# A two-block transformer kernel: the tail of the second block's mixing product, the query products of its expert layer and the first expert choice, reordered

## Chip, core and metric

The kernel runs on one core of a Trainium2 chip. The metric is the device time of one execution in microseconds. The engines are TensorE (PE), VectorE (DVE), ScalarE (ACT), GpSimd (POOL) and SyncE (SP); in the profile PEld is TensorE's loading of the stationary operand, which runs beside its products.

## What is computed

Two transformer blocks over 256 tokens of width 1024, in fp32. The change lies in the second block, from its output product on:

```
x = x + mixed @ w_out
hn = _rmsnorm(x, norm2_g)
q = (hn @ peer_wq).reshape(tokens, 8 heads, 256)
s1 = q[..., :128] . peer_keys[0]        # 128 scores
s2 = q[..., 128:] . peer_keys[1]        # 128 scores
v1, i1 = top_k(s1, 16);  v2, i2 = top_k(s2, 16)
cand_s = v1[:, None] + v2[None, :]      # 16 x 16 sums
top_s, pos = top_k(cand_s, 16)
e = i1[pos // 16] * 128 + i2[pos % 16]
g = softmax(top_s)
h = gelu(x . peer_u[e])
out = sum(g * h * peer_v[e])
x = x + out;  return _rmsnorm(x, final_g)
```

For each token and head 16 of 16384 experts are chosen, and for each of them a row of 1024 numbers of `peer_u` and one of `peer_v` are read from DRAM: 2 x 16 rows for each of 256 x 8 pairs, 268 MB in all.

## The kernel before

Tokens lie in two tiles of 128 (t = 0, 1), one token on a partition. All weights of the dense products come as granules of 1 MB (128 x 2048 fp32) through a ring of three slots: SP loads granule n into `raw[n % 3]`, ACT writes its high part `w_hi` (`prepare`, L1126), POOL writes the rest `w_lo` (`low_part`, L1998, in four pieces), and PE makes three fp32r products for one fp32 product: high x high, low x high, high x low (`mm3`, L612 to L614, and `by_parts`, L701 and L705). A slot is loaded again when its low part is written.

The output product of the second block uses four granules, `wp0` to `wp3` (`half_sum`), each for both token tiles; q is the granule, q % 2 the output half and q // 2 the half of the inner dimension. `wp2` and `wp3` also wait for the convolution branch (`conv_out`, written by DVE L1814). Results go to PSUM banks, DVE adds them to `X` (`residual`, L1458), PE transposes `X` (`raw_turn`, L681), DVE multiplies by the gain (L1451), ACT takes the high part (L1135) and DVE the low part (L1443).

Then follow eight query products, one for each head (`pair`, granules `wq0` to `wq7`, 48 products of 256 columns each), ACT's copy of each to `query` (L1320, L1326), the key scores (`score_tile`, L982) and ACT's copy of these to `match`. The low parts of the last five granules are made by DVE (`late_split`, L1931), all others by POOL.

A group g is one head of one token tile; there are 16, tile 0 first. For each, DVE chooses 16 experts (`choose_first` for group 0, `choose` for the others; the indices are written at L1872 and L1896), POOL issues 16 indirect DMAs for rows of `peer_u` and 16 for rows of `peer_v` (L2036, each fetches one 4 KB row for each of 128 tokens, 0.52 MB), in batches m = 0 to 7 of two rows, DVE makes the dot products with the u rows (L1913, 16 for a group), ACT the gelu and 16 diagonal matrices of weights (L1353, L1360), and PE adds the weighted v rows (L1008, 32 fp32 products of 512 columns, shown as 64 records). u rows and v rows have one buffer each: a u batch is fetched again when DVE has used it (`u_free`), a v batch when PE has (`v_free`).

POOL's order decides when rows come: u rows of group 0, u rows of group 1, then, after the last query product, v rows of group 0; from there on a loop over groups g = 2 to 15 with, for each m, the u batch of group g and the v batch of group g - 1. The first u batches of the loop wait for the choice of group 2, which DVE makes in the midst of the dot products of group 1.

## Time and profile before

| | us |
|---|---|
| median of 3 runs | 1361.41 |
| lowest and highest of them | 1357.44, 1363.77 |
| the profiled execution | 1354.4 |
| its span, first to last instruction | 1352.6 |
| mean granted clock of TensorE | 0.886 of 2.4 GHz |
| busy: PE, DVE, ACT, POOL | 1101.4, 714.1, 419.0, 895.2 |
| moved by all DMA | 356.86 MB, of it 268.47 MB by POOL's indirect DMAs |

All times in the rows below count from the start of the span, 1352.6 us long; 1.8 us of the execution lie around it. POOL's 512 indirect DMAs run from 571.5 to 1315.8 us, more than half of the span. A row of a timeline gives start, duration, engine, line, operation, output <- input, count, and in brackets the idle time before it with what ended it; "issue" and "remote" there mean that the profile shows nothing that it waited for. An fp32 product appears as two records, an fp32r product as one.

### The profile page before, as it was taken

To read this page: it belongs to the slowest core of one execution; us is meant where nothing else is said; L and a number is where in the kernel's file an instruction comes from. 1 tells how busy PE (TensorE), PEld (TensorE's weight loads), DVE (VectorE), ACT (ScalarE), POOL (GpSimd) and SP (SyncE) were. 2 spreads that over 40 slices of the span, in tenths; PEclk is the share of its full clock that TensorE was granted. 3 is DMA by queue.
4 is the path that set the end of the run, shared out by engine and by line. 5 is a ranking of instruction groups with operands and counts; after the bars stand their busy time and mean duration, and the time that the engine had idled before them with its cause. 6 is when DMAs were issued, how large, how long until landed. Compare 5 with 4: busy or idle time off the path is not lost.

```text
span 1352.6 us, 14212 instructions
## 1 busy us (share of the span) xinstructions
PE 1101.4 (81%) x4814; PEld 735.0 (54%) x4814; DVE 714.1 (53%) x1600; ACT 419.0 (31%) x761; POOL 895.2 (66%) x845
## 2 busy tenths in 40 slices
PE   6999999999999998996858757766877776686757
PEld 5778898999988877893313313322333232232322
DVE  6436222222263786594646567746665664572842
ACT  4355454444435445534202202220222022012202
POOL 5764448788897675686565757666766666765670
PEclk9999889999999999997988879768977877887878
DMA  7533225555554312499799999999999999989891
GB/s 253 182 129 121 77 84 187 171 178 179 179 190 179 109 48 100 161 373 350 304 389 350 365 370 366 352 352 408 348 346 360 382 359 350 411 339 366 310 410 65
DMA packets 89442, 356.86 MB, mean 264 GB/s; under 512 B 9648, under 2 KB 9776, under 8 KB 81840
## 3 DMA queue, kind: packets, MB, share of 16 engines
q0 software_dynamic: 73728, 268.47, 51.5%
q1 hardware_dynamic: 15232, 86.15, 17.9%
q10 hardware_dynamic: 432, 1.57, 0.4%
q8 instruction: 32, 0.52, 0.2%
q14 instruction: 18, 0.15, 0.0%
HBM read 355.10 MB, written 1.05 MB: 263 GB/s over the span
## 4 chain that ended last, share of the span: by engine, by line
PE 15%; DVE 12%; issue 10%; another core or an unknown queue 8%; POOL 3%; DMA 1%; ACT 1%; DVEq 0%; ACTq 0%; POOLq 0%
PE bank L1008 14%; DVE u_row L1913 7%; POOL v_row L2036 2%; POOL u_row L2036 2%; DMA v_row<-peer_v_dram,expert 1%; DVE gain L1843 1%; ACT diag L1360 1%; DVE gain L1894 0%; DVE c_part L1895 0%; DVE gain L1892 0%; DVE c_pos L1850 0%; DVE s_idx L1846 0%; DVE s_idx L1850 0%; DVEq L1392 0%
## 5 line engine op out<-in xcount | busy, mean ns | idle before, releaser
L1008 PE MATMUL bank<-v_row,diag 128*128 128x512 f32 x960 | 500.4, 669 | 197.2 <-issue 156.4
L1998 POOL TENSOR_TENSOR w_lo<-raw,w_hi 128x512 fp32r<-128x512 f32 x296 | 375.7, 1303 | 155.4 <-ACT w_hi L1126 155.0
L1008 PEld LDWEIGHTS bank<-v_row,diag 128*128 128x128 f32 x960 | 200.9, 212 | 496.4 <-issue 453.9
L1913 DVE CUSTOM_DVE_ANT_0 u_row<-u_row,bank 128x1024 f32<-128x1024 f32 x256 | 298.5, 1218 | 63.6 <-issue 52.3
L2036 POOL DMA_INDIRECT u_row<-peer_u_dram,expert x256 | 248.7, 972 | 113.5 <-issue 78.3
L2036 POOL DMA_INDIRECT v_row<-peer_v_dram,expert x240 | 226.7, 945 | 138.9 <-issue 67.3
L612 PE MATMUL bank<-hT_hi,w_hi 128*128 128x256 f32 x672 | 194.7, 290 | 5.2 <-issue 1.8
L614 PE MATMUL bank<-hT_hi,w_lo 128*128 128x256 f32 x672 | 192.6, 287 | 5.7 <-issue 5.7
L613 PE MATMUL bank<-hT_lo,w_hi 128*128 128x256 f32 x672 | 192.5, 286 | 2.4 <-issue 2.3
L1126 ACT ACTIVATE w_hi<-raw 128x2048 fp32r<-128x2048 f32 x79 | 150.9, 1911 | 109.0 <-PE bank L614 64.7
L1353 ACT ACTIVATE gelu<-dots 128x16 f32<-128x16 f32 x16 | 3.5, 216 | 476.5 <-DVE dots L1913 221.1
L612 PEld LDWEIGHTS bank<-hT_hi,w_hi 128*128 128x128 f32 x672 | 131.5, 196 | 10.9 <-issue 8.0
L614 PEld LDWEIGHTS bank<-hT_hi,w_lo 128*128 128x128 f32 x672 | 131.3, 195 | 5.2 <-issue 5.2
L613 PEld LDWEIGHTS bank<-hT_lo,w_hi 128*128 128x128 f32 x672 | 131.6, 196 | 1.3 <-issue 1.3
L1360 ACT ACTIVATE diag<-consts,mixw 128x128 f32<-128x128 f32 x256 | 77.3, 387 | 83.0 <-remote 55.7
L1708 DVE TENSOR_TENSOR full<-full,bank 128x512 f32<-128x512 f32 x11 | 7.6, 688 | 102.9 <-PE bank L614 102.9
L701 PE MATMUL bank<-w_hi,hT_hi 128*128 128x512 f32 (+2 forms) x128 | 46.4, 374 | 6.8 <-DVE hT_lo L1443 2.9
L701 PE MATMUL bank<-w_hi,hT_lo 128*128 128x512 f32 (+2 forms) x128 | 45.9, 370 | 0.0
L1882 DVE COPY gain<-match 128x256 f32 (+1 forms) x15 | 4.8, 322 | 74.1 <-remote 37.3
L1458 DVE TENSOR_TENSOR residual<-residual,bank 128x512 f32<-128x512 f32 x12 | 8.2, 684 | 61.5 <-PE bank L614 31.8
L612 PE MATMUL bank<-w_hi,ff_hi 128*128 128x512 f32 x88 | 34.3, 390 | 0.9 <-issue 0.9
L613 PE MATMUL bank<-w_lo,ff_hi 128*128 128x512 f32 x88 | 34.2, 389 | 0.0
(259 smaller groups left out, 1333.4 us busy)
## 6 DMA issues: line engine op xcount, KB each, us to landing
raw<-stream_dram SPq DMA_DIRECT2D x79, 1024.0 KB
u_row<-peer_u_dram,expert POOLq DMA_INDIRECT x256
v_row<-peer_v_dram,expert POOLq DMA_INDIRECT x240
residual<-x_in_dram SPq DMA_DIRECT2D x2, 512.0 KB, 4.6
out_dram<-residual SPq DMA_DIRECT2D x4, 256.0 KB, 2.1
consts<-consts_in_dram SPq DMA_DIRECT2D x1, 840.0 KB, 13.5
gain<-norm_final_dram ACTq DMA_DIRECT2D x1, 512.0 KB, 7.5
normed_tokens<-norm_g_dram ACTq DMA_DIRECT2D x1, 512.0 KB, 3.5
```

The lines of the kernel that those rows point to most:

```text
L612: mm(out_ap, left[0], right[0], start=first, stop=False, skip_group_check=resumed)
L613: mm(out_ap, left[0], right[1], start=False, stop=False, skip_group_check=resumed)
L614: return mm(out_ap, left[1], right[0], start=False, stop=last, skip_group_check=resumed)
L701: mm(outs[t], x[:, k, t * P:(t + 1) * P], w, start=first and k == chunks[0] and x is source[0], stop=False)
L1008: ins = mm(accs[half][:, :], diag[:, 2 * m + i, :], row[:, half * 512:(half + 1) * 512], start=False, stop=True, skip_group_check=True)
L1126: activation(w_hi[n % RING][:, :], raw[n % RING][:, :], ACT.Copy).then_inc(high_done, 1)
L1360: ins = activation(diag[:, i, :], ident, ACT.Copy, scale=mixw[:, i:i + 1])
L1458: ps.empty(v.tensor_tensor(part, part, bank[:, :], ALU.add), (name, t, half))
L1843: ins = v.match_replace(left, top[:, 0:8], values, TAKEN)
L1913: ins = v.tensor_tensor_reduce(out=row_of_u, in0=row_of_u, in1=hn_tile[:, :], scale=1.0, scalar=0.0, op0=ALU.mult, op1=ALU.add, accum_out= ...
L1998: ins = nc.gpsimd.tensor_tensor(w_lo[r][:, cols], raw[r][:, cols], w_hi[r][:, cols].bitcast(F32), ALU.subtract)
L2036: nc.gpsimd.indirect_dma_start(rows[2 * m + i][:, :], None, table_in, bass.IndirectOffsetOnAxis(ap=expert[:, b, 2 * m + i:2 * m + i + 1], ...
```

## The change

- **Order of the output product.** The pieces of `wp0` to `wp3` are now one for each granule and token tile. Those of tile 0 come first, with only `wp1`'s piece for tile 1 split around the transposes of tile 0. Norm, first query product and key scores of tile 0 stand between pieces of tile 1.
- **`wp3`'s high and low part** have a fourth slot, and ACT makes the high part just after the attention, ahead of the square root of the convolution branch.
- **Query products unsplit.** Granules `wq0` to `wq7` are neither split by ACT nor by POOL or DVE. PE multiplies fp32 weights with an fp32 `hT_whole`: 16 products of 128 columns for one head and tile (heads 0 and 1, `query_of_tile`), 16 of 256 columns for both tiles (heads 2 to 7, `query_of_head`). Each granule has a place of its own, and SP loads all before the first rows of experts are fetched.
- **First choice.** Group 0's first eight experts come from the sums of the eight best of each list (8 x 8 instead of 16 x 16). The first index is ready as soon as the two lists of eight are (`best_expert`), seven more after that, and the other eight after a residual addition of tile 1.
- **Gathers.** POOL begins with one u row, then one and fourteen more; v rows of group 0 for m = 0 and 1 come ahead of group 1's u rows, those for m = 2 to 7 behind, each batch m when the query product of head m is done (its weights lay there).
- **ACT's weights of group 0** (`expert_weights(0)`) stand between heads 4 and 5, and no longer behind head 7; DVE chooses group 2 as soon as the scores of head 2 are copied, and makes the dot products of group 1 after that without a break.

```
-LATE = 5
+NSPLIT = GRANULES.index("wq0")
...
-            for n in range(RING, NGRAN):
-                late = n - RING - (NGRAN - LATE)
...
+            for n in range(RING, NSPLIT):
+                sp.wait_ge(split_done, n - RING + 1)
                 load(n)
+                if GRANULES[n] == "wp2":
+                    ps.full(sp, ("conv", 3))
+                    load_query(5)
+            for h in range(RING):
+                sp.wait_ge(split_done, NSPLIT + h - RING + 1)
+                load_query(h)
+            sp.wait_ge(part_read, PARTIAL.index("wp0") + 1)
+            for h in (3, 4):
+                load_query(h)
+            sp.wait_ge(conv_out, 2)
+            for h in (6, 7):
+                load_query(h)
...
+            tile_of_out(0, 0)
+            partly_read("wp0", tile_of_out(0, 1))
+            ps.start(pe, ("out2", 0, 1))
+            tile_of_out(1, 0)
+            pe.wait_ge(conv_out, 2)
+            ps.fill(tile_of_out(2, 0), ("out2", 0, 0))
+            ps.fill(tile_of_out(3, 0), ("out2", 0, 1))
+            turn_of_out(0, 0)
+            ps.start(pe, ("out2", 1, 1))
+            out_products(1, 1, "high", range(2))
+            turn_of_out(0, 1)
+            query_of_tile(0, 0, fresh=True)
+            out_products(1, 1, "high", range(2, 4))
+            tile_scores(0, 0)
+            partly_read("wp1", out_products(1, 1, "low"))
+            ps.fill(tile_of_out(2, 1), ("out2", 1, 0))
+            ps.fill(tile_of_out(3, 1), ("out2", 1, 1))
+            turn_of_out(1, 0)
+            query_of_tile(1, 0)
+            turn_of_out(1, 1)
+            query_of_tile(0, 1, fresh=True)
+            tile_scores(1, 0)
+            query_of_tile(1, 1)
+            tile_scores(0, 1, freed=(experts_ready, 1))
+            for h in range(2, NH):
+                query_of_head(h)
...
+            for h in range(2, NH):
+                copy_query(h)
...
+                if h == 4:
+                    expert_weights(0, 0, first=True)
...
-            choose_first()
-            late_split(NGRAN - 5)
-            late_split(NGRAN - 4)
-            dve.wait_ge(match_done, 2)
+            v.memset(flag[:, :], 0.0).then_inc(u_free, BATCHES)
+            settle(v.memset(cand[:, 0, :], TAKEN))
+            for half in range(2):
+                residual("out2", parts=[(0, half)])
+            for half in range(2):
+                turned_gain(0, half)
+            token_rstd(0)
+            choose_eight()
+            residual("out2", parts=[(1, 0)])
+            choose_other_eight()
+            residual("out2", parts=[(1, 1)])
+            for half in range(2):
+                turned_gain(1, half)
+            token_rstd(1)
+            dve.wait_ge(gain2_done, 16)
+            for t in range(TT):
+                normed_tokens(t)
+            dot_products(0, range(0, 1))
+            dve.wait_ge(match_done, 1)
             choose(1, 1)
-            late_split(NGRAN - 3)
-            late_split(NGRAN - 2)
-            dot_products(0, range(0, 2))
-            late_split(NGRAN - 1)
-            dot_products(0, range(2, BATCHES))
+            dot_products(0, range(1, BATCHES))
             weights(0, 0)
-            dot_products(1, range(0, 4))
-            dve.wait_ge(match_done, TT * NH)
+            dve.wait_ge(match_done, 4)
             choose(2, 2)
-            dot_products(1, range(4, BATCHES))
+            dot_products(1, range(BATCHES))
             weights(1, 1)
...
+            pool.wait_ge(u_free, BATCHES)
+            pool.wait_ge(part_read, PARTIAL.index("wp1") + 1)
+            pool.wait_ge(best_expert, 1)
+            gather(peer_u, u_rows, u_in, 0, 0, pair=(0,))
+            pool.wait_ge(first_experts, 1)
+            gather(peer_u, u_rows, u_in, 0, 0, pair=(1,))
+            gather(peer_u, u_rows, u_in, 0, 1)
+            ps.full(pool, ("out2", 1, 1))
+            for m in range(2, BATCHES // 2):
+                gather(peer_u, u_rows, u_in, 0, m)
+            pool.wait_ge(experts_ready, 1)
+            for m in range(BATCHES // 2, BATCHES):
+                gather(peer_u, u_rows, u_in, 0, m)
+
+            def first_v(m):
+                ps.full(pool, ("query", m, 1) if m < 2 else ("query", m))
+                gather(peer_v, v_rows, v_in, 0, m)
+
+            for m in range(2):
+                first_v(m)
             pool.wait_ge(experts_ready, 2)
             for m in range(BATCHES):
                 fetch_u(1, m, BATCHES + m + 1)
-            ps.full(pool, ("query", NH - 1))
-            for m in range(BATCHES):
-                gather(peer_v, v_rows, v_in, 0, m)
+            for m in range(2, BATCHES):
+                first_v(m)
```

How the engines' rows move, first PE around the transposes of the output. `yT_hi` and `yT_lo` are the parts of the input of the output product, `residual` is `X`. Before:

```order
2607 L705 MATMUL bank<-w_lo_56,yT_hi 128x512 x4
2608 L681 MATMUL bank<-consts,residual 128x128 x4
2609 L681 MATMUL bank_7<-consts,residual 128x128 x4
2610 L701 MATMUL bank<-w_hi_53,yT_hi 128x512
2611 L701 MATMUL bank<-w_hi_53,yT_lo 128x512
...
2618 L705 MATMUL bank<-w_lo_56,yT_hi 128x512 x4
2619 L681 MATMUL bank<-consts,residual 128x128 x8
2620 L612 MATMUL bank<-hT_hi,w_hi_54 128x256
2621 L613 MATMUL bank<-hT_lo,w_hi_54 128x256
2622 L614 MATMUL bank<-hT_hi,w_lo_57 128x256
```

and the same engine after the change, from the last piece of tile 0 on:

```order
2592 L992 MATMUL bank<-w_lo_59,yT_hi 128x512 x4
2593 L1012 MATMUL bank<-consts,residual 128x128 x4
...
2598 L1012 MATMUL bank<-consts,residual 128x128 x4
2599 L1033 MATMUL bank<-hT_whole,raw_51 128x128 x16
2600 L994 MATMUL bank<-w_hi_54,yT_hi 128x512
...
2604 L1048 MATMUL bank<-params,query 128x128 x2
2605 L992 MATMUL bank<-w_lo_58,yT_hi 128x512 x4
2606 L994 MATMUL bank<-w_hi_52,yT_hi 128x512
```

The first query product and the first scores now stand ahead of 28 of tile 1's 48 products; before they stood behind all 96 and behind the product of both tiles. Second POOL, at the end of its splitting; before:

```order
60 L1998 TENSOR_TENSOR w_lo_56<-raw_50,w_hi_53 128x512 x4
61 L2036 DMA u_row_76<-peer_u_dram,expert 128x1024
62 L2036 DMA u_row_77<-peer_u_dram,expert 128x1024
...
93 L2036 DMA v_row_92<-peer_v_dram,expert 128x1024
94 L2036 DMA v_row_93<-peer_v_dram,expert 128x1024
```

and after:

```order
57 L2139 TENSOR_TENSOR w_lo_59<-raw_50,w_hi_55 128x512 x4
58 L2178 DMA u_row_83<-peer_u_dram,expert 128x1024
59 L2178 DMA u_row_84<-peer_u_dram,expert 128x1024
...
74 L2178 DMA v_row_99<-peer_v_dram,expert 128x1024
75 L2178 DMA v_row_100<-peer_v_dram,expert 128x1024
76 L2178 DMA v_row_101<-peer_v_dram,expert 128x1024
77 L2178 DMA v_row_102<-peer_v_dram,expert 128x1024
78 L2178 DMA u_row_83<-peer_u_dram,expert 128x1024
```

Four of the v rows moved ahead of group 1's sixteen u rows, and the last granule that POOL splits is now `wp3`, no longer `wq2`.

## Rows read from the trace of the kernel before

**Rows 1.** From the page: granted clock and DMA share in 40 slices.

```profile
PEclk9999889999999999997988879768977877887878
DMA  7533225555554312499799999999999999989891
```

**Rows 2.** POOL's timeline: the 48 gathers ahead of the loop, its first two groups.

```profile
571.52 1.15 POOL L2036 DMA_INDIRECT u_row<-peer_u_dram,expert  x1 [3.42 <-DVE expert L1872]
572.98 0.94 POOL L2036 DMA_INDIRECT u_row<-peer_u_dram,expert  x1 [0.30 <-issue]
...
624.15 0.94 POOL L2036 DMA_INDIRECT v_row<-peer_v_dram,expert  x1 [5.52 <-PE bank L614]
...
653.31 0.94 POOL L2036 DMA_INDIRECT u_row<-peer_u_dram,expert  x1 [9.55 <-DVE expert L1896]
...
696.46 0.94 POOL L2036 DMA_INDIRECT u_row<-peer_u_dram,expert  x1 [3.35 <-DVE dots L1913]
```

**Rows 3.** POOL's timeline in the loop: one group.

```profile
857.33 0.94 POOL L2036 DMA_INDIRECT v_row<-peer_v_dram,expert  x1 [6.23 <-remote]
...
903.29 0.94 POOL L2036 DMA_INDIRECT v_row<-peer_v_dram,expert  x1 [6.44 <-remote]
```

**Rows 4.** Stretches: length, busy PE, PEld, DVE, ACT, POOL, granted clock, DMA share, GB/s.

```profile
590.00:600.00 10.00, 10.00 (x87) 10.00 (x86) 9.94 (x12) 4.63 (x8) 8.43 (x6) 1.00 1.03 414
610.00:620.00 10.00, 2.92 (x8) 1.85 (x8) 2.84 (x6) 0.84 (x2) 6.58 (x7) 0.72 1.02 406
640.00:650.00 10.00, 10.00 (x25) 4.50 (x24) 5.78 (x29) 0.00 (x0) 2.84 (x4) 1.00 0.89 354
```

**Rows 5.** PE's timeline.

```profile
525.22 1.95 PE L862 MATMUL bank<-conv_a,consts 128*128 128x256 f32 x8
527.01 1.00 PE L846 MATMUL bank<-v,PT 128*128 128x64 f32 x8
...
536.28 1.98 PE L705 MATMUL bank<-w_lo,yT_hi 128*128 128x512 f32 x8
538.09 0.39 PE L701 MATMUL bank<-w_hi,yT_hi 128*128 128x512 f32 x1
...
615.94 0.37 PE L612 MATMUL bank<-hT_hi,w_hi 128*128 128x256 f32 x1 [1.04 <-issue]
```

**Rows 6.** ACT's timeline: the attention's end, copies of query products.

```profile
530.82 1.28 ACT L1054 ACT_TABLE_LOAD   x1
...
533.41 0.42 ACT L1295 ACTIVATE rstd_c<-rstd_c 128x256 f32<-128x256 f32 x1 [1.10 <-DVE little L1804]
...
540.09 1.92 ACT L1126 ACTIVATE w_hi<-raw 128x2048 fp32r<-128x2048 f32 x1 [0.29 <-issue]
...
605.98 0.60 ACT L1326 ACTIVATE query<-bank 128x512 f32<-128x512 f32 x1 [6.08 <-PE bank L614]
...
623.91 0.60 ACT L1326 ACTIVATE query<-bank 128x512 f32<-128x512 f32 x1 [12.06 <-PE bank L614]
```

**Rows 7.** DVE's timeline.

```profile
539.83 0.69 DVE L1814 TENSOR_TENSOR yT_lo<-conv_b,yT_hi 128x512 fp32r<-128x512 f32 x1 [0.96 <-ACT yT_hi L1304]
...
564.80 0.50 DVE L1840 MAX8 s_top<-bank 128x8 f32<-128x128 f32 x2 [1.59 <-PE bank L982]
...
579.05 0.28 DVE L1882 COPY gain<-match 128x256 f32<-128x256 f32 x1
...
587.65 0.18 DVE L1896 SCALAR_TENSOR_TENSOR expert<-c_part 128x16 uint32<-128x16 f32 x1
...
605.91 1.22 DVE L1913 CUSTOM_DVE_ANT_0 u_row<-u_row,bank 128x1024 f32<-128x1024 f32 x1
...
662.63 0.44 DVE L1882 COPY gain<-match 128x256 f32 x1 [0.41 <-issue]
...
689.44 0.18 DVE L1896 SCALAR_TENSOR_TENSOR expert<-c_part 128x16 uint32<-128x16 f32 x1 [0.71 <-issue]
...
889.16 1.22 DVE L1913 CUSTOM_DVE_ANT_0 u_row<-u_row,bank 128x1024 f32<-128x1024 f32 x1 [1.31 <-issue]
```

More of the change, by code:

```diff
@@ L980, in score_tile, with query_of_head @@
+            def query_of_head(h):
+                w = query_weights(h)
+                bank = ps.start(pe, ("query", h))
+                for c in range(2):
+                    for k in range(KD):
+                        ins = mm(bank[:, c * T:(c + 1) * T], w[:, k, c * P:(c + 1) * P], hT_whole[:, k, :], start=k == 0, stop=k == KD - 1)
+                ps.fill(ins, ("query", h))
             def score_tile(bank, h, t, at):
@@ L1292, in _ @@
             attention("G", 2, 0)
+            prepare("wp3")
             warm(ACT.Sqrt)
```

371 lines of the change are left out of this document (207 added, 164 removed).

## Prediction

> **What bounds the kernel now.** Read the page first: in its 40 slices the DMA share stands at 9 from the middle of the run to the end [rows 1], and POOL's indirect DMAs alone span from 571.5 to 1315.8 us. So the second half is a chain of gathers, and the question for any edit ahead of it is when the loop over groups can start. POOL's timeline answers it: the first gather at 571.52 waits for DVE's first indices, the first of the loop at 653.31 waits for DVE's indices of group 2 [rows 2]. Between them lie 48 gathers in 81.8 us, though POOL can issue one each 1.245 us (0.94 and 0.30 between them [rows 2]), 59.8 us for 48.
>
> Then look at one group of the loop. From 857.33 to 903.29 it takes 45.96 us for 32 gathers [rows 3]: 32 issues are 39.8 us, and ahead of the v batch POOL waits some 6 us more until PE has freed it. From 653.31 to 857.33 [rows 2, 3] POOL issued 142 gathers, 1.437 us each, the same pace as 45.96 / 32 = 1.436. So the loop runs at its own pace from its first group on, and what the change is worth is how much earlier than 653.31 it starts, as long as nothing inside it is altered. The loop's code is not.
>
> One more thing has to be seen, since it enters the sum. With the DMA share at 1.02 for long, PE and DVE slow down although nothing is waited for: in 610 to 620 us PE is busy 2.92 of 10 us [rows 4], with 1.04 us of idle time after each record of 0.37 [rows 5], where in 590 to 600 it made 87 records, 0.115 us each [rows 4]; and at 889 us the dot products on DVE have 1.31 us of unexplained idle time between them [rows 7]. I call it a slow spell. The first was there by 610, 38 us after the first gather, and ended once POOL had paused [rows 2]; in the loop one is there at 889, 32 us after POOL resumes at 857.33. The first stretched the last query product: its copy comes 17.9 us after the one before [rows 6], where 48 records and the scores (0.9) are 6.4. So 11.5 us were lost in a spell of 13, 0.88 of it.
>
> **The change, part by part.** Start to start on PE: eight fp32r products of 512 columns take 1.81 us [rows 5], 0.227 each; one piece of the output product (12) is 2.72. Four fp32 products of 256 columns (8 records) take 1.79 [rows 5], 0.45 each, so 16 of them, a head, 7.2; the trace has no fp32 product with these operands, this is the nearest row. Half the columns I take at half: 3.65 us for 16 products of 128 columns, with a little added for each record. Before, 48 split products cost 5.5 [rows 4]. So PE pays 1.7 us more for a head, some 13 us in all; this is the cost of the change, and below it lies on the path. If the records come as far apart as the 1.95 us that those eight take to their end allow, a head is 7.8 and six heads cost 3.6 more; it can hardly fall below 6.4, since 25 records of twice the columns fill 10 us at full clock [rows 4], 0.2 for a record of ours.
>
> *To the first gather.* PE starts at 532.6 as before. `wp3`'s high part, 1.92 us [rows 6], now goes ahead of the table load at 530.82; the square root, at 533.41 now, comes at 530.8 + 1.9 + 1.3 + 0.2 = 534.2, and the convolution branch, done at 540.5 [rows 7], at 541.4. Three pieces end at 540.8, so PE waits 0.6 us: its price. Two more pieces 546.9, transpose 0.5, half a piece 0.9, transpose 0.5 (these cover DVE's addition and gain), query of tile 0 3.65, half a piece 0.9 (covers ACT's copy), scores 0.5: DVE starts choosing at 554.1, where it stood at 564.80 [rows 7]. Two maxima 0.5 [rows 7], two index searches and a sum (together 1.4 by their share of the 6.3 that DVE took before, 564.80 to POOL's 571.52) make the best index at about 556.0, the first gather goes at 556.2, the second at 558.3. That is 15.3 us earlier than 571.52.
>
> *48 gathers.* The second to sixteenth u row, 15 x 1.245, reach 577.0, the four v rows 581.9. Their conditions are earlier: the other eight experts at about 564.5, tile 1's output pieces 560.2, query (0,1) 569.9, query (1,1) 574.0. Group 1's experts: DVE has residual, gains, two norms (1.3 each) and two dot products done by 571.7, and the choice takes 579.05 to 587.65 = 8.7 us [rows 7], so 580.4, in time. SP's weight loads, which shared the DMA with the first gathers, are all done by then; they are issued between about 480 and 542 us, where the DMA share was low [rows 1]. Group 1's u rows end at 601.8; they need DVE's dot products of group 0 (from 580.4 on, 1.22 us each [rows 7], two 2.44 against POOL's 2.49), which is just enough. v rows for m = 2 to 5 end at 611.8. Then PE decides: query 2 starts at 574.5, ends with its scores at 582.1; each further head is 7.2 + 0.9 for scores, so query 6 is done at 613.5 and query 7 at 621.6. POOL issues the last v pair 621.8 to 624.3, and the loop starts at **624.3** at the earliest. Group 2's experts are not late: ACT's weights of group 0 after head 4's scores (599), gelu 602.6, choice 8.7, so 611.6; its own copies for heads 5 to 7 are not delayed by it, since query 5 is done at 605.4 and ACT is free at 608.
>
> *The slow spell.* POOL now issues without a break from 558.3 on, so by both times seen (32 and 38 us) DVE and PE have slowed down by 590 to 596. DVE's dot products of group 0 then take some 2.5 us each in place of 1.22 [rows 7], POOL's u rows of group 1 wait for them, the DMA drains and the spell ends: some 8 us, in which PE loses 0.88 of the time as it did before, 7 us. That is on the path by queries 6 and 7. Bounds: nothing (loop at 624.3), or the same again while POOL runs free from 602 to 612 (some 16 us lost in all, 640). I take 7: loop at 631.3, which is **22 us** earlier than 653.31.
>
> *Off the path.* ACT loses eight high parts (15 us), DVE five low parts (2.3 each), POOL three; none ended a wait on the path except through the query products. DVE's smaller first choice counts in the 15.3 above.
>
> The sum against the profiled execution: span 1352.6 - 22 = 1330.6, time 1332. The profiled execution, 1354.4, lies 7.0 below the median of 1361.41; I take the difference to the median: 1361.4 - 22 = **1339.4**.
>
> **A rule weighed.** In slices with little PE work the granted clock stands at 0.7 to 0.8 [rows 1], and in the slow spell 0.72 [rows 4]; the two levels are 1.2 and 2.4 GHz. The Trainium skill (TensorE: Matmul & The Clock Gate, Part 1) says that the clock has just these two states and falls only when the array has been idle. By this the fp32 products, which keep PE busy, stay at the high level as in 640 to 650, and the sum stays; if it were wrong, the fourth rival below holds.
>
> **The rivals.**
>
> *Given back in the first groups.* Before, DVE began to choose group 3 at 662.63 [rows 7], 9 us after the loop's start, with PE done with group 0's v rows. Now PE begins these at the loop's start, 64 records at 25 in 10 us [rows 4] and two more products, 28 us, and the choice waits for them. It took 27 us before, slowed all the way (to 689.44 [rows 7]), and 8.7 us unslowed; here POOL stops at 40 us and so ends the slowing, and the choice is ready at about 50. Group 3's u rows, 43 us after the loop's start before (696.46 [rows 2]), come at about 52: 9 us lost, gain 13, and with a longer spell 7. Against it: the wait drains the DMA, so the next groups run faster, as 1.437 us for each gather over the first four groups shows that such delays are made up.
>
> *More than forecast.* If no spell occurs and the better filled buffers let two groups run at POOL's 39.8 us and not 46, the gain is 29 + 12 = 41. Against it: the 6 us wait is there on both sides of the group shown [rows 3].
>
> *No change.* The spell returns for each head: a head of 32 records at 0.7 us is 22 us. With four such heads after 590 us the loop starts near 653. Against it: POOL needs each query product for its next v pair, so it must pause.
>
> *Slower.* The granted clock stays at 1.2 GHz through the fp32 query products of heads 2 to 7: 6 x (14.4 + 1.8) = 97 us in place of 49, loop at 672, 19 us later than before: 1380. It makes the kernel measurably slower once over three quarters of that stretch are at the low level. For it: the clock falls in spells [rows 4]. Against: fp32 products at 1.00 at 640 to 650 [rows 4] and a busy PE at 590 to 600.
>
> **How the numbers follow.** Forecast (loop starts at 623 to 640, gain 13 to 30): 0.60. Given back (gain 7 to 13): 0.14. More (30 to 41): 0.08. No change: 0.10. Slower: 0.08. A difference of under about 0.5%, 6.8 us, can't be told from none here. Faster 0.82, same 0.10, slower 0.08. The range leaves out no change and slower (0.18): gain of 8 to 39 us, 1322 to 1354.
>
> **What would show it.** The first gather at 555 to 557 us and the sixteenth u row near 577; 32 PE records for a head in about 7.2 us at clock 1.00; POOL waiting for query 6 and 7 and for no other; the loop's first u row at 624 to 640; and 46 us for each group from there. If the heads take over 8 us at full clock, the fp32 price is wrong; if PE and DVE crawl from 585 on for over 10 us, the spell is undersized; if group 3's u rows come over 50 us after group 2's, the gain is given back there.

## The result, and the profile after

The changed kernel took 1361.88 us (median of 20 runs, 1358.67 to 1366.42), the kernel before, timed beside it, 1358.20 (20 runs, 1352.08 to 1366.22): a ratio of 1.0043, interval 1.0027 to 1.0060. So it is slower by some 0.4%, within the 0.5% that the prediction took as no change, and outside the predicted range of 1322 to 1354. Ratios, here and below, rest on the runs of each kernel that lie within 1.5% of its fastest and medians on all its runs, so that a ratio need not be the quotient of two medians. The profiled execution has a span of 1360.5 us where the one before had 1352.6.

POOL's timeline shows where it went. First the gathers ahead of the loop, to be laid beside [rows 2], then the first u gather of groups 3, 4 and 15 and of the last v rows:

```profile
552.09 1.25 POOL L2178 DMA_INDIRECT u_row<-peer_u_dram,expert  x1 [18.53 <-DVE expert L1990]
...
571.03 1.06 POOL L2178 DMA_INDIRECT u_row<-peer_u_dram,expert  x1 [0.31 <-issue]
575.29 0.94 POOL L2178 DMA_INDIRECT v_row<-peer_v_dram,expert  x1 [3.19 <-PE bank L1033]
...
585.05 0.94 POOL L2178 DMA_INDIRECT u_row<-peer_u_dram,expert  x1 [3.75 <-DVE expert L2032]
...
624.17 0.94 POOL L2178 DMA_INDIRECT v_row<-peer_v_dram,expert  x1 [8.38 <-PE bank L1043]
...
639.77 0.94 POOL L2178 DMA_INDIRECT v_row<-peer_v_dram,expert  x1 [5.62 <-PE bank L1043]
...
642.26 0.94 POOL L2178 DMA_INDIRECT u_row<-peer_u_dram,expert  x1 [0.30 <-issue]
...
694.33 0.93 POOL L2178 DMA_INDIRECT u_row<-peer_u_dram,expert  x1 [5.47 <-DVE dots L2049]
...
742.67 0.94 POOL L2178 DMA_INDIRECT u_row<-peer_u_dram,expert  x1 [8.83 <-DVE dots L2049]
...
1264.61 0.94 POOL L2178 DMA_INDIRECT u_row<-peer_u_dram,expert  x1 [7.86 <-DVE dots L2049]
```

The first gather is 19.4 us earlier than before (571.52), the loop's first, at 642.26, 11.1 us earlier (653.31), group 3's first, at 694.33, only 2.1 us earlier (696.46, [rows 2]). From there to group 15's first the changed kernel takes 570.3 us, 47.5 per group, the kernel before 559.9 (to 1256.38), 46.7 per group: the lead of 2.1 us turns into a lag of 8.2, and the spans differ by 7.9. So the gain is lost at three places: 8 us ahead of the loop, 9 us in its first round, 10 us over the twelve groups behind it.

Ahead of the loop it is slow spells on TensorE, twice. Its timeline (start, duration, line, product, count, idle time before):

```profile
560.62 2.02 PE L1033 MATMUL bank<-hT_whole,raw 128*128 128x128 f32 x16
569.95 0.58 PE L1033 MATMUL bank<-hT_whole,raw 128*128 128x128 f32 x1 [7.30 <-issue]
...
594.28 5.78 PE L1043 MATMUL bank<-hT_whole,raw_late 128*128 128x256 f32 x26
601.23 0.38 PE L1043 MATMUL bank<-hT_whole,raw_late 128*128 128x256 f32 x1 [1.17 <-issue]
602.62 0.38 PE L1043 MATMUL bank<-hT_whole,raw_late 128*128 128x256 f32 x1 [1.01 <-issue]
...
614.77 9.13 PE L1043 MATMUL bank<-hT_whole,raw_late 128*128 128x256 f32 x32
...
632.43 7.07 PE L1043 MATMUL bank<-hT_whole,raw_late 128*128 128x256 f32 x32
642.90 3.60 PE L1105 MATMUL bank<-v_row,diag 128*128 128x512 f32 x8
```

In the middle of one query product PE starts nothing for 7.3 us, with no releaser but "issue"; query 4 makes 26 of its 32 records by 600.1 and then one each 1.4 to 2.1 us, and query 5 starts at 614.77, 12.7 us late. DVE, ACT and PE are idle together for most of these stretches.

In the loop the spell falls on DVE's choice of the next group's experts. DVE's timeline, one choice of the steady loop:

```profile
947.96 0.46 DVE L2018 COPY gain<-match 128x256 f32 x1 [0.99 <-issue]
...
955.30 0.42 DVE L2020 TENSOR_TENSOR gain<-s_top 128x256 f32<-128x256 f32 x1 [3.66 <-remote]
...
965.09 0.09 DVE L1958 MATCH_VALUE_LOAD c_pos<-c_top,gain 128x8 f32 x1 [3.38 <-issue]
...
972.09 0.69 DVE L2028 TENSOR_TENSOR gain<-c_digit,consts 128x512 f32<-128x512 uint32 x1 [3.88 <-remote]
...
975.71 0.17 DVE L2032 SCALAR_TENSOR_TENSOR expert<-c_part 128x16 uint32<-128x16 f32 x1
```

This choice takes 27.9 us, and each one from group 4's on takes 26 to 29. In the kernel before the same instructions took 10.0 to 10.3 us in eight of the ten rounds behind 800 us: there POOL paused in the middle of a group for v rows [rows 3], DVE chose right behind the pause, and the spell hit the dot products instead [rows 7]. In the changed kernel the round closes over DVE, as POOL's timeline shows for two groups:

```profile
929.98 0.94 POOL L2178 DMA_INDIRECT u_row<-peer_u_dram,expert  x1 [8.10 <-DVE dots L2049]
...
979.02 0.94 POOL L2178 DMA_INDIRECT u_row<-peer_u_dram,expert  x1 [9.60 <-DVE dots L2049]
```

A group's first u row waits for the first two dot products, which DVE makes right behind its choice (it ends at 975.9, they at 978.2). From the end of a choice to the start of the next DVE takes 19.0 to 21.1 us, with hardly any waiting, so POOL is 18 us into its stream when DVE begins to choose, and the choice falls into the spell again: 27.9 and 19.0 us are this round.

### The profile page after: what moved, and what is told of

The parts are those of the page before. It is cut to its first block, busy times and chain, and to the rows that moved or that the text cites. A ratio compares the mean times of both kernels' runs of the same rounds, so it can differ in the third digit from the quotient of the medians.

```text
span 1360.5 us, 14035 instructions
## 1 busy us (share of the span) xinstructions
PE 1083.1 (80%) x4750; PEld 735.5 (54%) x4750; DVE 691.5 (51%) x1595; ACT 401.8 (30%) x749; POOL 870.3 (64%) x833
## 4 chain that ended last, share of the span: by engine, by line
DVE 24%; issue 12%; another core or an unknown queue 11%; PE 4%; DVEq 1%; DMA 0%; ACT 0%; POOL 0%; ACTq 0%; POOLq 0%
DVE u_row L2049 13%; PE bank L1105 4%; DVE gain L2028 1%; DVE c_part L2031 1%; DVE gain L1951 1%; DVE gain L2030 1%; DVE c_top L1948 1%; DVE gain L2020 1%; DVE s_idx L1954 1%; DVE s_idx L1958 1%; DVEq L1507 1%; DVE c_pos L1958 0%; DVE c_pos L1954 0%; DVE s_top L1948 0%
## 5 line engine op out<-in xcount | busy, mean ns | idle before, releaser
L1105 PE MATMUL bank<-v_row,diag 128*128 128x512 f32 x960 | 474.4, 652 | 217.5 <-issue 201.1
L2049 DVE CUSTOM_DVE_ANT_0 u_row<-u_row,bank 128x1024 f32<-128x1024 f32 x256 | 294.0, 1218 | 11.1 <-DMA u_row<-peer_u_dram,expert 11.0
L1226 ACT ACTIVATE w_hi<-raw 128x2048 fp32r<-128x2048 f32 x71 | 135.6, 1911 | 103.4 <-PE bank L667 64.7
L665 PE MATMUL bank<-hT_hi,w_hi 128*128 128x256 f32 x544 | 155.8, 286 | 3.3 <-POOL w_lo L2139 1.8
L667 PE MATMUL bank<-hT_hi,w_lo 128*128 128x256 f32 x544 | 154.6, 284 | 0.0
L666 PE MATMUL bank<-hT_lo,w_hi 128*128 128x256 f32 x544 | 154.6, 284 | 0.0
L665 PEld LDWEIGHTS bank<-hT_hi,w_hi 128*128 128x128 f32 x544 | 105.1, 193 | 5.5 <-POOL w_lo L2139 2.6
L666 PEld LDWEIGHTS bank<-hT_lo,w_hi 128*128 128x128 f32 x544 | 105.1, 193 | 0.0
L667 PEld LDWEIGHTS bank<-hT_hi,w_lo 128*128 128x128 f32 x544 | 105.0, 193 | 0.0
L1043 PE MATMUL bank<-hT_whole,raw_late 128*128 128x256 f32 x160 | 39.2, 400 | 7.8 <-issue 7.8
L1043 PEld LDWEIGHTS bank<-hT_whole,raw_late 128*128 128x128 f32 x160 | 31.9, 202 | 13.1 <-issue 8.8
## 6 DMA issues: line engine op xcount, KB each, us to landing
consts<-consts_in_dram SPq DMA_DIRECT2D x1, 840.0 KB, 11.1
```

Of the source, the lines that this page charges most:

```text
L665: mm(out_ap, left[0], right[0], start=first, stop=False, skip_group_check=resumed)
L666: mm(out_ap, left[0], right[1], start=False, stop=False, skip_group_check=resumed)
L667: return mm(out_ap, left[1], right[0], start=False, stop=last, skip_group_check=resumed)
L1043: ins = mm(bank[:, c * T:(c + 1) * T], w[:, k, c * P:(c + 1) * P], hT_whole[:, k, :], start=k == 0, stop=k == KD - 1)
L1105: ins = mm(accs[half][:, :], diag[:, 2 * m + i, :], row[:, half * 512:(half + 1) * 512], start=False, stop=True, skip_group_check=True)
L1226: activation(w_hi[parts_slot(n)][:, :], raw[n % RING][:, :], ACT.Copy).then_inc(high_done, 1)
```

## The experiments

Eighteen runs of fourteen different kernels, the two unchanged ones among them, were made in five sets, each set on one chip, with the kernel before timed beside. No kernel leaves out any of the computation. The chips turned out to be of two kinds, which decides how all the rest is read. I call them A (sets 1 and 2), B (set 3), C (set 4) and D (set 5). The kernel before took 1251.7 and 1253.1 us on A, but 1369.1, 1364.2 and 1368.8 us on B, C and D, with single runs from 1345 to 1378, as in the first timing (1352 to 1366).

### Pauses that were no pauses, on chip A

The edit, behind each four gathers of the loop, ahead of the loop behind each pair, or both:

```
+                nc.gpsimd.memset(pause_cell, 0.0).then_inc(paused, 1)
```

> The changed kernel, with one small POOL memset (128x8) behind every four gathers of the loop over groups; nothing is left out of the computation. Theory, slow spells from saturation: where gathers follow each other every 1.24 us for some 20 us, the transfer engines reach 405 to 420 GB/s with 4 to 5 gathers outstanding, and from then on DVE, PE and ACT start their instructions late, until POOL stops. In the changed kernel this falls on DVE's choice of the next experts (24 us instead of 10) and makes a group 47.5 us. A pause of 0.15 to 0.3 us per four gathers makes 32 gathers 41.0 to 42.2 us, keeps the transfers below saturation, and the choice is back at about 10 us: 13 groups from 694 at about 42 us each, the last one's rows as before, 1285 to 1310 us in all. Rival, the new places of the rows in SBUF or anything else that slows the loop by itself: the pauses come on top or change nothing, 47 to 50 us per group, 1358 to 1395 us. Rival two, a group is bound by the chain of DVE and PE work and not by transfers: the pause is taken out of POOL's wait, 47.5 us per group, 1360 us.

> The kernel before, with the same memset behind every four gathers of its loop; nothing is left out. Saturation theory: 41 to 42.2 us per group instead of 45.95, end at 1290 to 1315 us, and the changed kernel with the same pauses stays ahead of it by the 11 us by which its loop starts earlier (642.3 against 653.3), less what group 3 gives back (its rows came 52 us behind the loop's start, against 43), so by 2 to 11 us. Rival, the new places of the rows: this kernel and the changed one differ per group by the 1.5 us seen, with pauses too, and the changed one is behind. Rival two, the chain of DVE and PE bounds a group: 45.95 us per group and 1353 to 1358 us.

> The changed kernel, with one memset (128x8) behind every pair of gathers of groups 0 and 1 ahead of the loop, from the second pair on; the loop is untouched, nothing is left out. Saturation theory: PE's two stops there (7.3 us at 562.6, and about 12 us from 600 to 612 in the products of query 4) vanish or shrink to under 3 us together, queries 6 and 7 are done 14 to 19 us earlier, and the loop's first u row starts at 624 to 630 instead of 642.3. What it is worth at the end: the loop has its own rhythm of 47.5 us; group 3's rows come some 50 us behind the loop's start, so 1345 to 1352 us if nothing gives it back, 1353 to 1360 if the loop falls into a slower rhythm. Rival: the stops of PE come from the loads of the last query weights, or from PE's own instruction stream, and stay with the pauses: loop start at 640 or later, 1360 us or more.

> The changed kernel with the pauses of both runs, ahead of the loop and in it. Saturation theory: the two gains add: loop start 624 to 630, 41 to 42.2 us per group, end at 1270 to 1295 us. Rivals as in the two runs: where only one of them gains, this one is at that time; where the chain of DVE and PE bounds the loop, 1345 to 1360 us.

Measured: 1233.3 us (ratio to the kernel before 0.9858, 0.9838 to 0.9877), 1253.2 (1.0015, 1.0000 to 1.0030), 1234.1 (0.9866, 0.9843 to 0.9888) and 1234.5 (0.9866, 0.9846 to 0.9886). All times are below what was expected, and not by the pauses: a memset of 0.12 us fits into the 0.30 us that POOL leaves between two gathers, so four gathers took 4.98 us with it and 4.97 without, and the kernel before, unpaused, was at 1251.7 itself. These runs said nothing on pauses. They said that on this chip the loop goes at 40 us per group without help.

### The two kernels on chip A

> The kernel before, unchanged, for a trace on the chip on which the other kernels of this call run. In the first call the memsets fell into POOL's 0.30 us between two gathers (4.99 us per four gathers with one, 4.98 without), so they changed nothing, and yet the paused kernel before took 1253 us there and the unpaused one 1252, against 1358 us where it was first timed; no engine had a slow spell, at 410 GB/s and 5 gathers outstanding. Theory one, the slow spells of DVE, PE and ACT under saturated transfers are a property of the chip or of its moment: this kernel takes either some 1252 us with 39.9 us per group and no slow spell, or some 1355 us with 45.9 us per group and the spells, and all kernels of this call are alike in it. Theory two, the memset did cure the spells, though the unpaused kernel was timed at 1252 us too: this cannot hold if this run is at 1252 us with a trace free of spells.

> The changed kernel, unchanged. Theory one: where there are no slow spells its gain is that of the loop's start, some 20 us (641.5 to 619 in the first call): 1234 us against 1252, ratio 0.986; where the spells occur, the gain is given back, ratio 1.004 and 1362 us. Rival, the change itself is worth nothing and the pauses gave the 17 us of the first call: ratio 1.0 in either case.

Measured: 1251.4 us (ratio 0.9992, 0.9975 to 1.0010) and 1233.6 us (0.9856, 0.9826 to 0.9887): here the change gains 1.4%, spans 1252.1 and 1231.7. POOL's timeline, first gather, loop, group 3, of the kernel before:

```profile
573.55 1.15 POOL L2036 DMA_INDIRECT u_row<-peer_u_dram,expert  x1 [3.42 <-DVE expert L1872]
...
641.20 0.93 POOL L2036 DMA_INDIRECT u_row<-peer_u_dram,expert  x1 [0.30 <-issue]
...
681.23 0.94 POOL L2036 DMA_INDIRECT u_row<-peer_u_dram,expert  x1 [0.30 <-issue]
```

and of the changed kernel:

```profile
553.73 1.25 POOL L2178 DMA_INDIRECT u_row<-peer_u_dram,expert  x1 [18.53 <-DVE expert L1990]
...
618.75 0.94 POOL L2178 DMA_INDIRECT u_row<-peer_u_dram,expert  x1 [0.30 <-issue]
...
661.47 0.94 POOL L2178 DMA_INDIRECT u_row<-peer_u_dram,expert  x1 [0.30 <-issue]
```

The loop starts 22.5 us earlier, group 3 comes 42.7 us behind it and not 40.0, and then both run at 40.0 us per group: the gain of the start reaches the end. Three stretches, first of the changed kernel as first timed, then on chip A (length, busy PE, PEld, DVE, ACT, POOL, granted clock, DMA share, GB/s):

```profile
560.00:570.00 10.00, 2.66 (x21) 2.26 (x21) 1.24 (x4) 1.36 (x4) 7.56 (x9) 0.89 1.00 389
600.00:612.00 12.00, 3.14 (x7) 1.53 (x7) 0.76 (x2) 0.84 (x2) 7.43 (x8) 0.72 1.03 414
700.00:1200.00 500.00, 333.69 (x669) 139.35 (x670) 285.49 (x715) 87.58 (x231) 319.59 (x341) 0.83 0.92 355
```

```profile
560.00:570.00 10.00, 9.64 (x85) 9.24 (x84) 9.54 (x23) 2.15 (x6) 7.61 (x8) 1.00 0.96 367
600.00:612.00 12.00, 12.00 (x65) 10.77 (x64) 11.62 (x31) 5.49 (x16) 8.82 (x10) 1.00 1.03 409
700.00:1200.00 500.00, 363.08 (x784) 141.15 (x783) 325.52 (x780) 95.54 (x252) 376.43 (x400) 1.00 1.03 410
```

At a DMA share of 1.03 and some 410 GB/s, for 500 us on end and with the same program, chip A has no spell: PE has 65 records in 12 us where it had 7, and each choice in the long stretch takes 10.0 to 10.2 us. So loaded transfers alone don't make a spell; the chip has a part in it, or something that ran on it at the time, which no run here separates.

### Slower gathers and an early choice, on chip A and again on chip C

The slower gathers, 0.39 us of POOL behind each four gathers of the loop, and each pair ahead of it:

```
+                nc.gpsimd.tensor_scalar(pause_cell, pause_from, 1.0, None, ALU.mult).then_inc(paused, 1)
```

The early choice:

```
-                    dve.wait_ge(v_free, g * BATCHES - BATCHES)
+                    for m in range(BATCHES):
+                        dve.wait_ge(v_in[m], g * PAIR_IN - PAIR_IN)
```

> The changed kernel with a POOL tensor_scalar (128x64) behind every pair of gathers ahead of the loop and behind every four in it, long enough to outlast the 0.30 us between two gathers: by the row of 0.93 us for 128x256, 0.12 + 0.2 us, so some 0.2 us more for every four gathers, 1.30 us per gather, 41.5 us per group. Where there are no slow spells this costs 1.5 to 2 us per group, 1255 to 1265 us. Where they occur: if they come from transfers at their limit (1.28 us per gather), they go and this kernel is at 1255 to 1290 us while the changed kernel is at 1360; if they do not hang on the last per cent of the transfers, they stay, 1355 to 1385 us.

> The changed kernel, with DVE's choice of a group's experts in the loop waiting for the arrival of the v rows that the overwritten list named, not for TensorE to have added them. Nothing is left out. Choice of group 3 starts some 30 us earlier (DVE was idle from 647 to 681 there). Where there are no slow spells group 3's u rows follow group 2's by 39.9 instead of 42.8 us: 3 us or nothing. Where they occur: group 3's u rows at most 45 us behind the loop's start instead of 52, and the choice no longer falls into the late, slow part of every group: 46 us per group or less, 1335 to 1350 us; rival, the choice is slow wherever it stands, or other work is slow in its place, 47.5 us per group and 1353 to 1362 us.

On chip A: 1259.3 us (ratio 1.0064, 1.0044 to 1.0085) at 42.7 us per group, and 1235.9 us (0.9883, 0.9834 to 0.9932). Slower gathers cost what they add, 26 us more than the changed kernel's 1233.6; the early choice changes nothing where no spell is.

On chip C, with two more widths:

> The changed kernel with a POOL tensor_scalar (128x64, 0.39 us) behind every pair of gathers ahead of the loop and every four in it: 1.33 us per gather and 42.7 us per group, 1259 us where there are no slow spells (measured). If the kernel before is timed near 1252 us here, this repeats that and tells nothing new. If it is timed near 1360 us, the chip has the spells. Theory, spells come from transfers at their limit of 1.28 us per gather: at 1.33 the backlog never forms, DVE's choice is at 10 to 12 us, a group takes 42.7 us and the kernel 1255 to 1270 us, 7% faster than the kernel before. Rival, spells come at any steady stream of gathers: 47 to 50 us per group, 1360 to 1400 us.

> The same with 128x32 in place of 128x64, some 0.1 us shorter: 1.30 us per gather, 41.7 us per group, 1243 to 1250 us where there are no spells. Where they occur: the theory of the transfers' limit has the threshold at 1.28 us per gather, so none here either, 1240 to 1255 us; if spells come in part, when single transfers are late, 1260 to 1340 us; rival as above, 1360 us or more.

> The kernel before with the 0.39 us of POOL behind every four gathers of its loop, none ahead of it. Without spells 1275 to 1285 us (1252 plus 14 groups of 2.8 us, less what POOL waited anyway). Where they occur: by the transfers' limit the loop is free of them from group 3 on, only those ahead of the loop stay (some 12 us): 1280 to 1300 us, so that the changed kernel with the same gathers is some 20 to 35 us ahead, its gain restored. Rival, the gain was never there on such a chip: the two are within 8 us.

> The changed kernel with DVE's choice in the loop waiting for the arrival of v rows instead of for TensorE. Where there are no spells 1234 us (measured). Where they occur: theory, the choice is made while the transfers are not yet saturated and a group falls to 46 us or less with group 3's rows at most 45 us behind the loop's start: 1330 to 1350 us; rival, in the steady loop DVE goes straight from the dots to the choice and waits for nothing, so the early wait alone is worth the 7 to 10 us of group 3 and the groups stay at 47.5 us: 1350 to 1358 us.

Measured: 1352.3 us (ratio 0.9976, 0.9912 to 1.0039), 1358.9 (1.0027, 0.9977 to 1.0077), 1359.1 (1.0024, 0.9969 to 1.0078) and 1360.4 (1.0002, 0.9931 to 1.0072). None can be told from the kernel before. The theory that a spell needs gathers faster than the transfers carry (1.28 us each) fell: at 1.33 us per gather seven of fourteen choices still took 17 to 25 us, at 1.31 us twelve of them 20 to 28 us, and the groups took 47.4 and 46.4 us. The early choice had 46.1 us per group with choices of up to 34 us in its trace: a slow choice does not by itself make a group 47.5 us. What the early wait did change is the first round: group 3's first u row stands 45.3 us behind the loop's start, and not some 52.

### Which part of the change brings the gain, and more load, on chip B

V rows last:

```
-            for m in range(2):
-                first_v(m)
...
-            for m in range(2, BATCHES):
-                first_v(m)
+            ps.full(pool, ("query", NH - 1))
+            for m in range(BATCHES):
+                gather(peer_v, v_rows, v_in, 0, m)
```

More load, on SP once group 2's experts are there, 60 times:

```
+                sp.dma_start(spent[:, 0:512], stream[0][:, 0:512]).then_inc(extra, 16)
```

The old choice puts the kernel before's first choice of experts back, in two halves around DVE's addition, and POOL's first wait is for eight experts and not for the best one.

> The changed kernel, with the 16 v rows of group 0 gathered as in the kernel before: all behind query 7, not each pair behind its own query. Nothing is left out. The prediction held that the gain is how much earlier the first gather starts (20 us in the traces of this chip) and counted on the v rows interleaved with the queries. Theory one, the loop's start is set by query 7 (done at 616 us in the changed kernel), not by the first gather: with the v rows last POOL idles from the end of group 1's u rows (599 us) to 616 and then needs 20 us, the loop starts at 636 to 638 instead of 619, and 15 to 18 of the 20 us go: 1248 to 1252 us. Rival, the first gather carries it and the order of the v rows is worth the 4.7 us that POOL waits for query 7 at most: 1234 to 1239 us.

> The changed kernel, with the first choice of experts made as before: both top lists of 16, 16x16 sums, eight experts with one-hot rows of 16, and POOL waiting for all eight at the first gather. Nothing is left out. First gather some 4 to 5 us later (by the two traces 8.7 us against 4 from the scores to the first gather). Theory one, the loop's start is set by query 7: POOL's wait for query 7 (4.7 us) shrinks by as much, the loop starts at 619 to 620, 1233 to 1235 us, the same as the changed kernel. Rival, the first gather carries the gain: 1238 to 1240 us.

> The changed kernel, with 60 further loads of 128x512 (256 KB, one after the other) into SBUF that nothing reads, from the time when group 2's experts are known: 15.7 MB, 38 us at 410 GB/s. Theory one, slow spells are a property of the chip or its moment: transfers that are asked for more than they can carry only take longer, 1265 to 1280 us, and DVE's choice stays at about 10 us. Theory two, the spells come with the depth of the backlog, and this chip has a somewhat higher threshold: DVE's choice stretches beyond 15 us, PE falls below 1.5 products per us, and the time is beyond 1290 us.

Measured: 1392.8 us (ratio 1.0161, 1.0121 to 1.0200), 1379.4 (1.0082, 1.0048 to 1.0116) and 1382.9 (1.0087, 1.0056 to 1.0118). The numbers expected were for chip A, so the places within the traces and the differences within the set count. With the v rows last (POOL's timeline):

```profile
555.55 1.15 POOL L2178 DMA_INDIRECT u_row<-peer_u_dram,expert  x1 [20.17 <-DVE expert L1990]
...
644.00 0.94 POOL L2178 DMA_INDIRECT v_row<-peer_v_dram,expert  x1 [31.09 <-PE bank L1043]
...
663.88 0.94 POOL L2178 DMA_INDIRECT u_row<-peer_u_dram,expert  x1 [0.30 <-issue]
```

The first gather stands some 16 us earlier than in the first trace of the kernel before [rows 2], yet POOL waits 31 us for query 7 and the loop starts at 663.9, 14.8 us behind the old choice's 649.1; at the end it is 13.4 us behind it. So the early first gather is worth little by itself: what lets the loop start early is that each v pair goes out behind its own query. The old choice starts gathering at 559.08, 2 to 4 us behind the other two of the set, and its loop starts at 649.1 where the loaded kernel's starts at 652.6: the shortened first choice has no share that shows, as expected of a loop that starts behind query 7. The changed kernel itself was not run on this chip, and between the traces of one kernel with spells the loop's start differs by 4 us (642.3 and 646.6), so a small share isn't ruled out. More load brought choices of 27 to 32 us, little above the 27 to 30 of the other two, and 3.6 us over the old choice in all. It can't speak on chip A's threshold, since it met a chip that has spells anyway.

### Gathers slow enough, and three kernels side by side, on chip D

The first has the tensor_scalar over 256 columns and not 64:

```
-        pause_cell, pause_from = turn_tab[:, 0, 0, 0:64], turn_tab[:, 1, 0, 0:64]
+        pause_cell, pause_from = turn_tab[:, 0, :, :], turn_tab[:, 1, :, :]
```

> The changed kernel with a POOL tensor_scalar of 128x256 (0.93 us) behind every pair of gathers ahead of the loop and every four in it: 1.45 us per gather, 355 GB/s, 46.4 us per group. Without slow spells 1300 to 1315 us. Where the kernel before is near 1360 us (a chip with spells): theory, spells need transfers that are busy nearly without a break, so none here, DVE's choice at 10 us in every group, 1300 to 1320 us, 3 to 4% faster than the kernel before; rival, they come with any long stream of gathers, DVE's choice again at 20 to 30 us, 1365 us or more.

> The changed kernel, unchanged. With spells: 47.5 us per group, the choice at 26 to 30 us in each group from the fourth on, ratio to the kernel before 1.000 to 1.008. Without: ratio 0.985, the choice at 10 us.

> The changed kernel with DVE's choice in the loop waiting for the arrival of v rows instead of for TensorE. With spells: if the rhythm of a group hangs on where the choice stands, 46 us per group and 12 to 18 us less than the changed kernel beside it; rival, the two are within 4 us, since spells take their time from whatever runs in them. Without spells: equal to the changed kernel within 3 us.

Measured: 1326.8 us (ratio 0.9806, 0.9724 to 0.9889), 1376.4 (1.0162, 1.0107 to 1.0217) and 1367.7 (1.0061, 1.0020 to 1.0103). For the last two that is 0.6% over and 0.1% under the kernel before by the medians of all runs. At 1.45 us per gather the spells are gone on a chip that has them. Its three stretches:

```profile
560.00:570.00 10.00, 9.49 (x83) 9.09 (x83) 9.47 (x19) 2.15 (x6) 8.69 (x9) 1.00 0.93 331
600.00:612.00 12.00, 12.00 (x65) 10.79 (x64) 11.37 (x39) 7.15 (x23) 10.18 (x12) 1.00 0.88 305
700.00:1200.00 500.00, 356.67 (x693) 137.87 (x691) 296.00 (x704) 79.86 (x210) 404.80 (x429) 0.92 0.97 360
```

and its loop (POOL's timeline):

```profile
636.78 1.00 POOL L2197 DMA_INDIRECT u_row<-peer_u_dram,expert  x1 [0.16 <-issue]
...
683.16 1.00 POOL L2197 DMA_INDIRECT u_row<-peer_u_dram,expert  x1 [0.17 <-POOL turn_tab L2193]
```

Each choice takes 10.0 to 10.6 us, PE has 65 records in 600 to 612 as on chip A, and POOL's waits in the loop are no longer than its usual 0.3 us. It is 3.6% faster than the changed kernel beside it, of which the steady groups, 46.6 us against 48.0, give only a part: 9.8 us are won up to the loop's start, 6.0 in the first round, 17 over the next twelve groups and some 15 behind them. The first of these is time that the two spells took ahead of the loop, less what the slower gathers cost there. It beats both kernels on this chip with spells. It was not run on chip A, where 0.39 us per four gathers cost 26 us, and the kernel before was not run with gathers each 1.45 us: how much of the 3.6% needs the change, and whether the change gains again once the spells are gone on such a chip, stays open.

The early choice beside the changed kernel gained 8.7 us, with single runs from 1355 to 1377. That is between the 12 to 18 expected if the place of the choice decided and the 4 of the rival, so its share stays open. Its trace, of one of its two slowest runs, speaks for the rival in the steady loop: 48.2 us per group, with choices of 27 to 33 us from group 4's on. DVE gets there late by its own work, so that an earlier wait moves nothing. Only the first round is shorter, 46.0 us against the changed kernel's 52.3 beside it.

## Why the prediction was wrong, point by point

**What bounds the kernel** held: a chain of gathers, and on chip A it is that and nothing else, at 40.0 us per group.

**To the first gather** the sum was right in its parts and wrong at its start. DVE began to choose at 549.64, 4.5 us ahead of the 554.1 forecast, and the gather went at 552.09 and not 556.2, because PE's first piece ran at 527.83 and not at the 532.6 that I had carried over from before; from there to the choice it took 21.8 us where the sum had 21.5. The convolution's sum over its channels had moved too, from 525.22 [rows 5] to 520.61. Most of that is luck of the execution. SP's timeline shows the same weight loads of the first block, far ahead of the change, in the kernel before and then in the changed one:

```profile
214.22 206.20 SPq L574 DMA_DIRECT2D raw<-stream_dram  x36
```

```profile
210.84 206.19 SPq L614 DMA_DIRECT2D raw<-stream_dram  x36
```

3.4 of the 4.6 us stood there already, and three other traces of the kernel before have 211.7 to 212.4 at this place; the other 1.2 us can come from the reordering (2.4 us by the two traces of chip A). From the choice to the gather it took 2.5 us and not 2.1. The sum's own additions are off by little: its terms give 553.9 and not 554.1 for the choice, and, from query 2's start at 574.5, 622.2 and not 621.6 for query 7.

**The fp32 heads** held: 32 records are 7.07 us long, a head with its scores follows the last in 7.80, against 7.2 and 0.9. The rule of the Trainium skill (TensorE: Matmul & The Clock Gate, Part 1) that the clock falls only when the array has been idle agrees with the rows: the granted clock is 1.00 from 579 to 600 us, through two heads and more, and 0.72 in 600 to 612, where PE was busy 3.14 of 12 us. The rival that was slower by the clock did not come.

**The sum of the 48 gathers** was some 6 us too careful without spells: query 7 was done at 615.8 us on chip A and the loop started at 618.75, where I had 621.6 and 624.3. PE's earlier start (529.47 there, not 532.6) explains half of it, and heads 7.80 us apart in place of 8.1 another 1.6.

**The slow spell** is the first step that failed, as a size. I gave it one occurrence and 7 us on PE, with 16 us in all as the bound; it came twice, at 562.6 for 7.3 us, only 10 us after the first gather, and at 600, for a loss of 12.7. The loop started at 642.3, past my outer 640. I had taken the time from the start of the stream to the spell, 32 to 38 us, from two cases of before, and nothing bears it out.

**Given back in the first groups**, the rival at 0.14, came in full: group 3's first u row stands 52.1 us behind the loop's start, and I had written about 52. DVE was idle from 647 to 681 us, waiting for PE to free the v rows, which PE could only begin at 642.90. Its gain of 13, or 7 with a longer spell, was then reckoned from the wrong start; from the real one 2.1 us were left. The round is 12.3 us longer than 32 gathers: 5.2 us are POOL's wait at group 3's first u row, behind DVE's late choice, and the other 7.1 are two waits ahead of v rows. The early choice bears this out: with it the first round took 45.3 us on chip C and 46.0 on D, and not 52. On chip A the 2.7 us lost are another wait, POOL's for PE to free the first v pair:

```profile
623.78 0.94 POOL L2178 DMA_INDIRECT v_row<-peer_v_dram,expert  x1 [2.86 <-PE bank L1105]
```

DVE's wait cost nothing there: the early choice began 20 us sooner, and group 3 still came 42.5 us behind the loop's start.

**The loop runs at its own pace** is the step that failed in kind. I took 45.96 us per group as a property of the loop, since its code was unchanged. It is a property of the chip, and, as the traces read, of where in a group the spell falls: 40.0 us on A for both kernels, 46.7 for the kernel before and 47.5 and 48.0 for the changed one on chips with spells. It lost 10.4 us here, more than the 7.9 by which the spans differ. In the changed kernel the place holds itself: a slow choice of 28 us and 19 us of dot products are the round, and the first gather of a group waits for the choice. That the entry into the loop decides which of the two rounds a kernel falls into is argued from the traces and not shown: the run that was to show it, the early choice, had 46.1 us per group in its trace on chip C and 48.2 in that on chip D.

What was right in the end is the mechanism on a chip without spells: the loop starts earlier by 22.5 us and 18 to 20 us arrive at the end, where I had 22. Nothing in the trace of before could say that such chips exist, but it did show spells in the loop as well, and the forecast left them out of the part of the sum where they mattered.

## What to carry to other kernels

The pace of a loop that shows unexplained idle time on several engines can't be carried over: here an unchanged body ran slower after an edit ahead of it, with its waits at another place in the round, and the time gained by starting it earlier was lost. Before costing such an edit, find which work the slow stretch falls on and what it would fall on if the round were shifted; and ask whether the stream that goes with the slow stretches may run slower, for a gather every 1.45 us beat one every 1.245 by 3.6%. Time the pair on more than one chip: here one change was worth 1.4% on one and cost 1.6% on another (0.6% by the medians of all runs).

## What the runs showed of the hardware that was not expected

Chips differ in whether PE, DVE and ACT have slow spells under a stream of gathers. On A the kernel before takes 1252 us and on three others 1345 to 1378, 7 to 10% more, with much the same transfers in the stream (409 to 410 GB/s on A, 406 to 414 in the stretches shown from the first timing). A was used twice within some ten minutes and the others once each, so it isn't shown that the chip itself and not its state at the time decides. With a gather every 1.245 to 1.33 us the spells are there on such chips, at 1.45 us (360 GB/s, chip D alone) they are not. Between 1.33 and 1.45 nothing was run, nor was anything that tells load from regularity: the slower stream also has 0.9 us of other work behind every four gathers.

In a spell instructions start on a grid of 0.70 us: PE's records from 601.23 to 612.41 start 1.39, 2.10, 1.40, 2.11, 2.09 and 2.09 us apart, and in the kernel before DVE's last dot products start at 883.56, 885.66 and 889.16. What an engine lacks in a spell stays open. The profile shows no data or buffer that it waits for ("issue" or "remote" stands as the releaser), nor a fetch of instructions that the transfers show. In 700 to 1200 us of the changed kernel's first trace the instruction queues carried one packet each (queue, kind, packets, MB, share):

```profile
q8 instruction: 1, 0.02, 0.0%
q14 instruction: 1, 0.01, 0.0%
```

The Trainium skill (Runtime: NRT & Kernel Launch, Instruction fetch mechanics) says that a jump to code outside the fetched pages costs a fetch over the transfers; by these two rows that is not what the loop's spells are made of. Another page of the Trainium skill (NOTIFIC — the notification-queue block, 7.1) says that the block that writes out the engines' records holds an engine back rather than lose a record on the way; no run here tests whether that plays a part.
